# Low parts of the weights by ScalarE and an accumulating transfer instead of a VectorE subtraction

## What is computed

```python
x = x + 0.5 * swiglu_ffn(rms_norm(x, ffn1_norm), ffn1_w_in, ffn1_w_out)      # D_FF = 2816
h = rms_norm(x, mix_norm)
q, k, v, xr, gate = split(h @ w_in_proj)                                     # 5 parts of 512
y_attn = diff_attention(q, k, v, ...)      # 4 heads, two softmax maps each
y_rnn  = rg_lru_branch(xr, gate, ...)      # conv of width 4, gates, scan
x = x + concatenate([y_attn, y_rnn]) @ w_out_proj
x = x + 0.5 * swiglu_ffn(rms_norm(x, ffn2_norm), ffn2_w_in, ffn2_w_out)
```

## Time and profile before

| | |
|---|---|
| median of 3 runs | 938.45 us (938.32 to 938.91) |
| profiled execution, its own time | 938.35 us |
| its span | 936.5 us |
| busy: TensorE / VectorE / ScalarE / GpSimd | 922.3 / 482.4 / 331.1 / 3.1 us |
| granted TensorE clock | 1.000 of full speed |
| loaded from HBM | 86.74 MB |

### The profile page before, as it was taken

One profiled execution on the slowest core, in us unless ns is written; L12 is line 12 of the kernel. 1 busy time (PEld: TensorE's weight loads), 2 busy tenths in 40 slices (PEclk: granted clock), 3 DMA queues, 4 the chain that ended last, 5 costly groups with the idle time before them and its releaser, 6 DMA issues.

```text
span 936.5 us, 11101 instructions
## 1 busy us (share of the span) xinstructions
PE 922.3 (98%) x4154; PEld 754.2 (81%) x4154; DVE 482.4 (52%) x712; ACT 331.1 (35%) x526; POOL 3.1 (0%) x25
## 2 busy tenths in 40 slices
PE   8999999999999999999997999999999999999998
PEld 7888888888888888777885678888888888888887
DVE  6754444444444346665879776645444444422221
ACT  7422222332223233356647654332222233211220
POOL 0000000000000000000000000000000000000000
PEclk9999999999999999999999999999999999999999
DMA  7222222222222224222221022322233222132241
GB/s 272 97 90 95 113 106 90 90 90 76 90 95 92 92 95 154 97 83 90 91 90 45 1 91 70 111 90 90 90 105 119 90 90 76 63 122 92 92 140 42
DMA packets 16295, 89.13 MB, mean 95 GB/s; under 512 B 2064, under 2 KB 2192, under 8 KB 8976
## 3 DMA queue, kind: packets, MB, share of 16 engines
q1 hardware_dynamic: 16128, 88.32, 27.1%
q0 software_dynamic: 144, 0.52, 0.2%
HBM read 86.74 MB, written 2.10 MB: 95 GB/s over the span
## 4 chain that ended last, share of the span: by engine, by line
PE 95%; DVE 2%; ACT 1%; DMA 1%; issue 1%; SPq 0%; ACTq 0%
PE bank L975 31%; PE bank L977 30%; PE bank L976 30%; PE bank L1172 1%; PE bank L1115 1%; PE bank L1149 1%; DMA raw<-w_in_dram 1%; PE bank L1162 0%; PE bank L1089 0%; DVE h_lo L599 0%; DVE small L896 0%; ACT w_hi L341 0%; PE bank L990 0%; ACT sq L518 0%; DVE yr_lo L803 0%
## 5 line engine op out<-in xcount | busy, mean ns | idle before, releaser
L975 PE MATMUL bank<-h_hi,w_hi 128*128 128x512 f32 x768 | 301.4, 392 | 0.9 <-DVE w_lo L587 0.8
L977 PE MATMUL bank<-h_hi,w_lo 128*128 128x512 f32 x768 | 298.9, 389 | 0.0
L976 PE MATMUL bank<-h_lo,w_hi 128*128 128x512 f32 x768 | 298.9, 389 | 0.0
L587 DVE TENSOR_TENSOR w_lo<-raw,w_hi 128x1024 fp32r<-128x1024 f32 (+1 forms) x178 | 188.7, 1101 | 79.5 <-ACT w_hi L341 73.9
L341 ACT ACTIVATE w_hi<-raw 128x1024 fp32r<-128x1024 f32 (+1 forms) x178 | 160.9, 951 | 159.9 <-PE bank L977 159.9
L975 PEld LDWEIGHTS bank<-h_hi,w_hi 128*128 128x128 f32 x768 | 144.1, 188 | 32.9 <-DVE w_lo L587 1.2
L976 PEld LDWEIGHTS bank<-h_lo,w_hi 128*128 128x128 f32 x768 | 144.2, 188 | 30.9 <-issue 1.2
L977 PEld LDWEIGHTS bank<-h_hi,w_lo 128*128 128x128 f32 x768 | 144.2, 188 | 30.1
L975 PE MATMUL bank<-act_hi,w_hi 128*128 128x512 f32 x352 | 136.9, 389 | 0.0
L976 PE MATMUL bank<-act_lo,w_hi 128*128 128x512 f32 x352 | 136.9, 389 | 0.0
L977 PE MATMUL bank<-act_hi,w_lo 128*128 128x512 f32 x352 | 136.9, 389 | 0.0
(11 more groups left out here) (173 smaller groups left out, 656.7 us busy)
## 6 DMA issues: line engine op xcount, KB each, us to landing
raw<-w_in_dram SPq DMA_DIRECT2D x43, 1024.0 KB, 4.8
raw<-w_out_dram SPq DMA_DIRECT2D x32, 704.0 KB, 4.0
raw<-w_qkv_dram SPq DMA_DIRECT2D x6, 1024.0 KB, 4.8
raw<-w_rnn_dram SPq DMA_DIRECT2D x4, 1024.0 KB, 4.7
raw<-w_proj_dram SPq DMA_DIRECT2D x4, 1024.0 KB, 4.8
x<-xT_dram SPq DMA_DIRECT2D x8, 256.0 KB, 6.0
out_dram<-x SPq DMA_DIRECT2D x8, 256.0 KB, 5.0
raw<-w_in_dram SPq DMA_DIRECT2D x4, 256.0 KB, 6.0
```

What stands on the lines that cost most here:

```text
L587: dve.tensor_tensor(w_lo[:, part], raw[:, part], w_hi[:, part].bitcast(F32), ALU.subtract).then_inc(low_made, 1)
L975: pe.matmul(dst, s_hi, m_hi, start=first, stop=False)
L976: pe.matmul(dst, s_hi, m_lo, start=False, stop=False)
L977: return pe.matmul(dst, s_lo, m_hi, start=False, stop=last)
```

## The change

ScalarE now writes minus the high part, -raw rounded to fp32r, into `w_lo` in two halves, and only then the two halves of `w_hi`. GpSimd waits for each half of minus (`minus_made`) and issues a transfer from `raw` to `w_lo` within SBUF that adds what it carries to what lies there, so that `w_lo` ends as raw minus high part. It is counted per slot in `low_landed`. TensorE and SyncE's loads wait for `high_made` and `low_landed` where they waited for `low_made`. VectorE's `lows` are gone everywhere. The first chunk's quarters are as before. GpSimd issues all 178 transfers in order; the load of `bd` and its later constants stand between those of chunk C_RNN and C_RNN + 1. TensorE waits for a whole chunk also in the first step of the second FFN, where it waited by halves.

```diff
@@ SyncE
                 if not first:
-                    sp.wait_ge(low_made, c * 2 - 2)
+                    sp.wait_ge(high_made, c * 2 - 2)
+                    sp.wait_ge(low_landed[slot], LANDED(c - 2, slot))
@@ GpSimd
+            def lows(first, last):
+                for c in range(first, last):
+                    slot, size = c % 2, OUT_COLS if C_OUT1 <= c < C_RNN or c >= C_OUT2 else IN_COLS
+                    for j in range(2):
+                        part = slice(slot * SLOT + j * size // 2, slot * SLOT + (j + 1) * size // 2)
+                        pool.wait_ge(minus_made, 2 * (c - 1) + j + 1)
+                        pool.dma_start(w_lo[:, part].bitcast(F32), raw[:, part], accum_op=ALU.add).then_inc(low_landed[slot], 16)
+            lows(1, C_RNN + 1)
             pool.wait_ge(chunk_used, USED(C_RNN - 1))
             pool.dma_start(bd[:, :], bd_in).then_inc(bd_landed, 16)
...
+            lows(C_RNN + 1, C_OUT2 + FFN_OUT)
@@ ScalarE, highs
-                for j in range(2):
-                    part = slice(slot * SLOT + j * size // 2, slot * SLOT + (j + 1) * size // 2)
+                halves = [slice(slot * SLOT + j * size // 2, slot * SLOT + (j + 1) * size // 2) for j in range(2)]
+                for part in halves:
+                    act.activation(w_lo[:, part], raw[:, part], ACT.Copy, scale=-1.0).then_inc(minus_made, 1)
+                for part in halves:
                     act.activation(w_hi[:, part], raw[:, part], ACT.Copy).then_inc(high_made, 1)
@@ VectorE
-            def lows(c, slot, size):
-                for j in range(2):
-                    part = slice(slot * SLOT + j * size // 2, slot * SLOT + (j + 1) * size // 2)
-                    dve.wait_ge(high_made, c * 2 + (j + 1))
-                    dve.tensor_tensor(w_lo[:, part], raw[:, part], w_hi[:, part].bitcast(F32), ALU.subtract).then_inc(low_made, 1)
...
@@ TensorE
+            def split_done(c, slot):
+                pe.wait_ge(high_made, c * 2 + 2)
+                pe.wait_ge(low_landed[slot], LANDED(c, slot))
...
-                        if f == 1 and k % (KT // 2) == 0:
-                            pe.wait_ge(low_made, 2 * c0 + 1 + k // (KT // 2))
+                        if f == 1 and k == 0:
+                            split_done(c0, 0)
...
-                    pe.wait_ge(low_made, i * 4 + 2 * ((C_IN1, C_IN2)[f] + s + 1))
+                    split_done(i * 2 + ((C_IN1, C_IN2)[f] + s), s)
```

More of the change, by code:

```diff
@@ L200, in build @@
         low_made = sem("low_made")
+        minus_made = sem("minus_made")
+        low_landed = [sem("low_landed0"), sem("low_landed1")]
         chunk_used = sem("chunk_used")
@@ L244, in USED, with LANDED @@
             return c + 3
+        def LANDED(c, slot):
+            return c * 16 + 16 * slot
         def tile_done(eng, done, s, t):
@@ L279, in _ @@
             sp.dma_start(rows[:, :], rows_in).then_inc(params_landed[1], 16)
+            sp.wait_ge(quarter_low, 2)
+            sp.wait_ge(low_made, 2)
             with sp.Fori(1, FFN_IN // 2) as i:
@@ L612, in ffn_in_step @@
                 part = slice(s * SEQ, (s + 1) * SEQ)
-                if size_next:
-                    lows(n + (C_IN1, C_IN2)[f] + 1, 1 - s, size_next)
                 if meanwhile:
@@ L631, in ffn_out_pair @@
                 for j in range(4):
-                    if sizes[j]:
-                        lows(i * 4 + ((C_OUT1, C_OUT2)[f] + j + 1), 1 - j % 2, sizes[j])
                     if meanwhile and j in meanwhile:
@@ L719, in ffn @@
                     add_square(k, k % 2)
-                lows((C_IN1, C_IN2)[f] + 1, 1, IN_COLS)
                 for k in range(EARLY_SQUARES, KT if f == 0 else 0):
                     add_square(k, k % 2)
-                lows((C_IN1, C_IN2)[f] + 2, 0, IN_COLS)
                 reciprocal_root((1, 3)[f])
@@ L748, in _ @@
             ffn(0, MIX_COLS)
-            lows(C_RNN + 1, 1, IN_COLS)
             reciprocal_root(2)
@@ L812, in _ @@
                 take_gate(t)
-                lows(C_RNN + t + 2, t % 2, IN_COLS if t < 2 else MIX_COLS)
                 convolve(t)
@@ L816, in _ @@
                     variance(t - 1)
-            lows(C_QKV + 2, 0, MIX_COLS)
             variance(RT - 1)
@@ L865, in _ @@
             qk_scale(0, qn, ROW_QG)
-            lows(C_QKV + 3, 1, MIX_COLS)
             rotate(0, qn)
-            lows(C_QKV + 4, 0, MIX_COLS)
             scan(0)
@@ L871, in _ @@
             qk_scale(1, kn, ROW_KG)
-            lows(C_QKV + 5, 1, MIX_COLS)
             rotate(1, kn)
             turned_heads(qT, 0)
-            lows(C_PROJ, 0, MIX_COLS)
             scan(2)
@@ L930, in _ @@
                     y_lows(2 * u + 1)
-                if u == RT:
-                    lows(C_PROJ + 1, 1, MIX_COLS)
                 if u - 1 in PROJECT_STEPS and PROJECT_STEPS.index(u - 1) % 2:
@@ L945, in _ @@
                 projected(j)
-                if j == lows_at:
-                    lows(C_PROJ + 2, 0, MIX_COLS)
             for h in range(HEADS):
@@ L953, in _ @@
                 projected(j)
-            lows(C_PROJ + 3, 1, MIX_COLS)
             for k in range(KT):
-                if k == KT // 2:
-                    lows(C_PROJ + 4, 0, IN_COLS)
                 if k % 4 < 3:
@@ L1040, in ffn @@
                         s, half = j // 2, j % 2
-                        pe.wait_ge(low_made, i * 8 + 2 * ((C_OUT1, C_OUT2)[f] + j + 1))
+                        split_done(i * 4 + ((C_OUT1, C_OUT2)[f] + j), half)
                         if half == 0:
@@ L1066, in token_chunk @@
                 c = C_QKV + 2 * s + half
-                pe.wait_ge(low_made, 2 * (c + 1))
+                split_done(c, half)
                 for t in range(TT):
@@ L1095, in recurrent @@
                 if gate == 0:
-                    pe.wait_ge(low_made, 2 * (C_RNN + t + 1))
+                    split_done(C_RNN + t, t % 2)
                     if t >= 2:
@@ L1180, in project @@
                 if jj == 0:
-                    pe.wait_ge(low_made, 2 * (C_PROJ + q + 1))
+                    split_done(C_PROJ + q, q % 2)
                 if j == 0:
```

## The result

The changed kernel takes 1001.34 us (median of 4 runs, 991.29 to 1004.08) against 938.68 us for the kernel before (4 runs, 938.32 to 939.67) on the same chip: a ratio of 1.065, 95% interval 1.058 to 1.071. The forecast was 969 us, so the sign and the range held and the size did not: 62.7 us were added where the sum said 30.5. The profiled execution took 1001.86 us, its span 1000.1 us; what follows is read from that one. Why another execution took 991.29 us, at no higher mean granted clock (0.986 against 0.990), no trace shows.

A forecast was written before the change was run, and what follows sets the result against it. TensorE bounds the kernel, with VectorE's subtractions beside its work. Added waits of 4 + 14.1 + 1.9 + 6.5 + 1.5 + 2.5 = 30.5 us on 938.35 us give 969 us, range 943 to 1045.

The forecast's parts named there:

- Input phases, 4 us: Both FFNs' input phases: split of 8.96 us ready at 119.16, due at 118.95; 0.1 us in each of 38 steps.
- First output phase, 14.1 us: First FFN's output phase: odd chunks' splits, begun behind a step's activation, late by 1.75 us for 7 and 1.9 for one.
- Second output phase, 1.9 us: Second FFN's output phase: splits ready 7.1 us after a chunk's end, due at 7.48; only the first odd chunk late, 1.9 us.
- Start, 6.5 us: Kernel start: TensorE gets chunk 1 at 25.03 instead of 19.57, 5.5 us, and chunk 3 is 1 us late.
- Attention, 1.5 us: Attention unit 4: ScalarE's two more halves stand ahead of unit 5's exponentials; between 1.2 and 1.9 us, 1.5 taken.
- Second FFN's first chunk, 2.5 us: Second FFN's chunk 1: ScalarE reaches it at 578.68, ready at 587.64, TensorE wants it at 585.14; 2.5 us late.
- Recurrent stage, "have cover": Recurrent and q, k, v stages: splits begin with a chunk's end and have 10.9 us or more for 9; no loss.
- Cheap: Rival for every transfer: data at the lower end, splits of 6.07 or 5.0 us, FFNs in time; 943.5 us, chance 0.22.
- dear transfers: Rival for every transfer: data at 4.5 and 3.1 us, splits of 12.8 and 9.8 us; about 1090 us, chance 0.25.
- GpSimd as the bound: Rival: issuing an accumulation holds GpSimd, or its queue fills, for over 5.4 us; over 1100 us, chance 0.04.
- not slower: Rival: VectorE's relief counts in attention, up to 0.8 + 2.4 us return; 935 us, chance 0.07.
- If even output chunks wait too, the data price was too low: Sign for the profile after: waits at even output chunks, or input steps late by a microsecond, mean data cost over 2.56 us.

The follow-up runs named there:

- the kernel with small loads: Changed kernel, but loads of the w_out chunks carry 88 of 1408 columns (products left wrong), all waits, splits and transfers kept; 981.79 us, ratio 1.046.

## Why the prediction came out as it did

**The mechanism and the sign were right.** TensorE had no reserve to give, VectorE's relief was worth nothing by itself (938.82 us with four fifths of its subtracting gone), and the new split is longer than the time TensorE leaves it. The steps, one by one:

1. *Input phases, 4 us*: wrong in kind. The steady step has a split of 8.3 us, not 8.96, and is 0.4 us in time, not 0.2 late; it costs some 0.02 us. Of what was lost there, 0.6 and 2.0 us, 1.9 us sit in three single steps (11.13, 11.82 and 11.54 us). That it comes near 4 us is chance. The price behind it: a split of 704 KB took 6.6 us (294.10 to 300.73 in the kernel with small loads) for a forecast of 7.09. Less the first minus halves that is 7.2 and 5.8 us; the 320 KB between them make 1.4 us, so 2.3 us per 512 KB where 2.56 was said (q0's 42.9% of 1000.1 us over 83.37 MB gives 2.70 us of engine time), and about 2.6 us are left as fixed, 2.75 by the forecast. The Trainium skill, "Collectives: The Full Stack", Part 3, has a reducing transfer at half the rate of a copy; the trace agrees, 2.70 us of engine time for 512 KB against the 1.51 us of the earlier trace rows for loads from HBM.
2. *First output phase, 14.1 us*: 17.5. A typical pair of chunks takes 16.75 to 16.85 us, 1.8 more than before, and 1.75 was said, but "even chunks are ready 0.4 us early" was wrong: it is mostly they that wait, for a transfer that met a load, and the odd ones are covered by that. The forecast's own cause was there too, and showed (1.27 us) once the loads were gone. The rest is the last pair but one, 19.65 us: a table load stands ahead of ScalarE's split (at 362.53, the split at 364.02), and the wait of 2.7 us that follows brings the half clock at 370.4. The table load is there in the kernel before too (at 341.6), and the forecast priced all odd chunks alike.
3. *Second output phase, 1.9 us*: 21.9. **This is the step that failed.** It took the load for something that "moves while no accumulation does". Its own numbers were against it: the load waits for the second transfer's landing, forecast 7.1 us after the chunk's end, and TensorE ends the next chunk at 7.48, so that load and next split were due within half a microsecond of each other. The forecast used the landing and the end for the question "in time?" and never for "at the same time as what?". Taking the loads away gave 18.6 us back. The last pair, 19.7 us where the others take 17.1 to 18.4, met the stores of the result besides, which the forecast didn't count either.
4. *Start, 6.5 us*: 9.0 with chunk 3. TensorE takes chunk 1 at 25.02 instead of 19.57, 5.45 us later, as said (5.5). Chunk 3's wait was 1.64 us for a forecast of 1, and its step took 1.9 us longer. The 1.6 us between them are the half clock behind the first wait.
5. *Attention, 1.5 us*: 4.9 with the projection. The wait was right at its upper end (1.9 us); the half clock and a wait of 0.8 us in the projection, where the forecast had none, came on top.
6. *Second FFN's first chunk, 2.5 us*: 0.55, TensorE's wait at 623.60. The split took 8.3 us (615.20 to 623.51), and it began 4.1 us behind TensorE's first matmul of the stage instead of 5.5: VectorE, which no longer subtracts at 566.29, ends its part of the projection sooner, and ScalarE's split stands behind that. It is the one place where the relief counted. The chunk behind it met a load (transfers issued at 623.63 and 624.58 land after 9.2 and 10.7 us) and waited 0.7 us, so that the stage lost 1.8 us in all.
7. *Recurrent stage, "have cover"*: 5.9 us. The cover was 10.9 us for a split of 9, and the split took 12.8 (387.46 to 400.3) beside a load. The same failed step as 3.

Against the spans the sum lacked 33.1 us: 20.0 and 5.9 us for the failed step, 3.4 in the first output phase, 3.4 in attention and projection and 2.5 at the start, less 1.4 in the input phases and 0.7 at the second FFN's start, which it had too high.

**The rivals.** Cheap and dear transfers both assumed one price for every phase, and so did the forecast between them. A split of 8.3 us alone lies nearer the forecast's 8.96 than the cheap 6.07; beside a load a small chunk took 9.5, nearly the dear rival's 9.8. That form, one price for all, was the mistake. GpSimd as the bound fell (0.85 to 1.24 us per issue), and "not slower" with it: its point was chunk 1's transfers landing within 1.6 us of its first minus half, and they landed 5 and 7.4 us after it (at 22.45 and 24.93).

**What the list of signs said.** "If even output chunks wait too, the data price was too low" was read off wrongly in advance: they did wait, in both output phases, and the data price was right. The sign was good, its reading lacked the load.

## What to carry to other kernels

When a transfer takes over an engine's work, ask of each point at which it starts what else that same semaphore releases: two users of the DMA engines that one event lets go start together as long as nothing stands ahead of one of them, and can then lock themselves in step, as in the second output phase. A buffer that is handed on later (here the raw slot, freed by a landing instead of an instruction's end) moves the load behind it, and pushing the load aside lengthens the chain if there are only two slots. And where TensorE fills the span, a long wait (here 2.3 to 5.7 us) may cost some 1.7 us on top of its length for the clock behind it, and in a stage with waits of its own much less (0.2 us for 6.8 us of half clock, in attention); in try-outs begin with the stage of the shortest period, which here held two thirds of the loss. And take a stage's end from the engine that bounds it: by VectorE's instructions attention and projection would have seemed to lose 3.5 us, where TensorE lost 4.9.

## What the chip showed that was not expected

- GpSimd spends 0.85 to 1.24 us on the issue of an accumulating transfer; of a pair of 512 KB the first lands after 4.5 us and the second, queued behind it, after 6.1.
- Beside a load of 704 KB, transfers of 352 KB took 6.3 to 8.3 us (880 to 960 us) instead of 3.7 to 5.1; beside one of 1024 KB, 512 KB took 9.0 and 10.5 instead of 4.5 and 6.0. The queues are different ones, SyncE's and GpSimd's; the engines are the same. The Trainium skill, "DMA: Bandwidth & Descriptors", section "Issuing engines are not separate DMA queues", says that transfers issued by different engines interleave on the same 16 engines; the trace agrees.
- TensorE's granted clock fell to 1.2 GHz for 3.4 or 6.8 us in or behind waits of 2.3 to 5.7 us, and in attention also where the waits in sight were no longer than 1.4 us. It didn't fall in the profiled execution of the kernel before, but by their mean granted clock it did in most of the others.
